# One core, two blocks: layer 1's keys projected for two heads at once, rarer modulation turns, early ScalarE tables, last sums read in place

## The chip, the cores and the metric

The kernel runs on one core of one Trainium2 chip, as a single launch. The metric is the device time of the launch in microseconds (us). Five engines of the core work side by side: TensorE (PE in the profile, with its weight loads as PEld), VectorE (DVE), ScalarE (ACT), GpSimd (POOL) and SyncE (SP), which here only issues the weight transfers.

## The reference

The computation is two model blocks on 256 image tokens ("x") and 256 context tokens ("ctx"), all in float32 with 1024 features. The first block has two layers:

```python
# layer 0: HGRN2 scan in two directions + differential attention, then a routed
#          mixture of 16 experts (top 2) for x and ctx
# layer 1: attention with a window, then a routed mixture for x alone
def odd_layer_mixer(h, hc, w_qkv, w_out, sink, rope, need_ctx):   # layer 1
    p = h @ w_qkv                                  # 16 query heads, 4 key, 4 value heads of 64
    q = p[..., :q_cols].reshape(b_, t_, C_HEADS, C_HEAD_DIM)
    k, v = jnp.split(p[..., q_cols:], 2, axis=-1)
    kvc = hc @ w_qkv[:, q_cols:]                   # context: keys and values alone
    kc, vc = jnp.split(kvc, 2, axis=-1)
    q = apply_axial_rope(q, cos, sin)              # x * cos + rotate_half(x) * sin
    k = apply_axial_rope(k, cos, sin)              # not for kc
    ...                                            # softmax with a sink over kc and a window of k
```

Each layer's norms are modulated by twelve rows that come from `silu(c) @ ada_w` for x and for ctx (shift, scale and gate of mixer and MoE). The second block is a mixer (state space scan and Fourier terms, with a gated norm) and an FFN with experts that choose their tokens. Its result is the last line that matters here: the sum over the experts' tokens goes through an RMS norm (square, mean, root), is multiplied by a gate row and added to x.

## The kernel before

The program of each engine is written out by hand, with a semaphore for each hand-over. Nothing reorders it: an engine runs its instructions in the order in which the code was written, and a wait holds back all that stands behind it on that engine. Stages end at a `meet()`, where PE, ACT and DVE wait for each other.

**Weights.** They stream from HBM through a ring of five slots of 2 MB in SBUF (more in the stages of experts). A piece is 1024 rows by 512 columns of a weight (`piece(key)`), `landed(n)` says that it is there, and SP issues the next transfer (L375) when the slot's last piece has been used up (`used.sem`, read as `consumed`). So the order of the pieces is fixed, and when one is used sets when the slot's next transfer starts.

**HGRN stage** (`hgrn_tensor`, `hgrn_vector`, `hgrn_scalar`). Two directions, four steps each (a step is 128 tokens), are written in turns with the layer's modulation: `in_turns(a, b, mods(...))` takes one turn of each in rotation. For PE a full step has 14 turns: 0, 1 and 10 hold no products of the scan, 2 to 9 hold one level of scores each, 11 the outputs, 12 the transposes, 13 the new state; the last step ends after its turn 11. The modulation is a chain of four units (`u` = 2 to 5). A unit has pieces of `ada_w` (one piece: 8 products of 32 x 512 that go through four column groups of PE) and then one block of sums: DVE copies the four partial sums out of PSUM (L656), PE adds them by two small products, DVE multiplies (L659), and a transfer queued on ACT writes the row out. There are 20 pieces and 4 blocks of sums in all. `mods(one, us)` gives a piece or a block of sums each turn, so that pieces stand at turns 0 to 3, 5 to 8, 10 to 15 and 17 to 22, and sums at 4, 9, 16 and 23: 12 pieces in the first step, 8 in the second, none in the last two.

**Layer 1's projection** (`qkv_tensor`, `qkv_scalar`, `qkv_vector`). `HT` holds the normed activations with features on partitions. PE makes units `u` of eight products into `bank(u % 4)`: units 0 to 7 are queries (two heads of 64 features in the 128 partitions), 8 to 11 keys, 12 to 15 values. A query head in the upper 64 partitions needs its key in the upper half too, so each key unit makes one head's key twice, into partitions 0 to 63 and 64 to 127, by two rounds of eight products that are 64 wide. ACT copies every unit out of PSUM. Between the units PE multiplies queries and keys of x by the rotation matrix (`rope`), and DVE adds up the turned parts (L2311 to L2313). The window attention follows after a `meet()`; it starts with products of `KK` and `QC`.

**Activation tables.** ACT has one set of functions loaded. The compiler puts an ACT_TABLE_LOAD directly ahead of an activation whose function isn't in the set. Whether it runs while ACT would wait for that activation's input, or only behind the wait, is seen in the trace by the idle time ahead of the load and behind it.

**Norms.** `normed(...)` makes squares on ACT, mean on DVE, root on ACT (L489), reciprocal on DVE (L514), then the scaled rows, transposes on PE and modulation. Between layer 1 and the second block `last_norm_vector` / `last_norm_scalar` scale x once more, and the second block's norm `norm2` squares all four chunks of x and ctx (L487).

**Last experts** (`experts_tensor`, `experts_scalar`, `experts_vector`). Pieces of three expert weights stream with wide slots, for four groups of tokens `g`. The sums over experts stay in four PSUM banks over all groups. At the end ACT and DVE copy them to SBUF (L3401, L3428), PE spreads the gate row over 128 partitions by two products (`gate_spread`), ACT squares (L3407) and takes the root (L3409), DVE scales and adds (L3435, L3437), and the result is stored.

## Time and profile before

| what | value |
|---|---|
| timed runs | 3090.97, 3085.37 and 3090.32 us, median 3090.32 us |
| profiled execution | 3081.36 us, of which the span of the engines is 3079.9 us |
| mean granted TensorE clock | 0.913 |
| PE busy | 81% of the span |
| DVE, ACT, POOL busy | 39%, 29%, 3% |
| DMA packets | 819.43 MB, mean 266 GB/s |
| HGRN stage | 142.5 to 333 us |
| layer 1's projection | 1235 to 1332 us |
| layer 1's experts | 1510 to 2010 us |
| last experts | 2587 us to the end |

The table's last rows are places on the time axis of the profiled execution. Rows of the trace give, for a group of instructions, the busy time, the mean duration of one and the idle time ahead of it on its engine with what ended it; rows of the time line give start and duration, and in brackets the idle time before. One float32 product shows as two records on PE (x16 is eight products).

### The profile page before, as it was taken

The page shows a single profiled execution, that of the slowest core. Times are in us where ns is not written, and L with a number is a line of the kernel's source. Part 1 is how long each engine was busy: PE and PEld are TensorE (multiplying, and loading weights), DVE is VectorE, ACT ScalarE, POOL GpSimd, SP SyncE. Part 2 cuts the span into 40 slices and gives each one's busy share as a digit, 9 for nine tenths or more (in the row PEclk, how much of TensorE's full clock was granted, in tenths as well). Part 3 has the DMA queues.
Part 4 walks back from the last instruction along what each step waited for, and adds up shares of the span by engine and source line. Part 5 has one row for each costly group of instructions (what it writes and reads, how often), then busy time and mean ns, then how long its engine had stood idle before and what let it go on. Part 6 is the DMA issues. An engine that isn't in the chain of part 4 may idle for free.

```text
span 3079.9 us, 30001 instructions
## 1 busy us (share of the span) xinstructions
PE 2498.3 (81%) x12205; PEld 1413.4 (46%) x12205; DVE 1207.3 (39%) x2040; ACT 895.6 (29%) x1408; POOL 107.7 (3%) x177
## 2 busy tenths in 40 slices
PE   6875687689999995998587777759898997778777
PEld 4734565578888884543232222234464433222222
DVE  2367537479999995153200000022661012000001
ACT  3334313278887784132100000032131011000000
POOL 1010300100000001000100000000000000000000
PEclk9986798889999997998799999969999998999998
DMA  9393530289999994373799999952102434999996
GB/s 341 123 363 147 201 144 1 95 319 393 389 394 395 393 378 179 132 259 132 274 399 403 398 402 403 372 178 82 41 20 96 164 132 176 409 409 409 409 409 279
DMA packets 246852, 819.43 MB, mean 266 GB/s; under 512 B 11075, under 2 KB 11241, under 8 KB 246448
## 3 DMA queue, kind: packets, MB, share of 16 engines
q1 hardware_dynamic: 226688, 753.88, 63.5%
q0 software_dynamic: 14432, 45.54, 4.3%
q10 hardware_dynamic: 5584, 17.98, 1.5%
q8 instruction: 101, 1.65, 0.2%
q14 instruction: 47, 0.39, 0.0%
HBM read 779.46 MB, written 37.90 MB: 265 GB/s over the span
## 4 chain that ended last, share of the span: by engine, by line
PE 58%; DMA 25%; DVE 10%; ACT 3%; issue 3%; SPq 1%; POOL 0%; DVEq 0%; ACTq 0%; POOLq 0%
PE PS L245 56%; DMA ring<-in_moe_w_up 8%; DMA ring<-in_w_e_down 4%; DMA ring<-in_w_e_up 4%; DMA ring<-in_moe_w_gate 3%; DMA ring<-in_w_e_gate 2%; DMA ring<-in_ada_w 1%; PE PS L1803 1%; DMA ring<-in_moe_w_down 1%; DVE hgrn L949 1%; SPq L375 1%; PE PS L551 0%; DVE SM L1412 0%; DVE SM L2415 0%; DMA row<-YP,DST 0%
## 5 line engine op out<-in xcount | busy, mean ns | idle before, releaser
L411 DVE TENSOR_TENSOR cut<-ring,cut 128x1024 fp32r<-128x1024 f32 x424 | 501.6, 1220 | 178.7 <-ACT cut L403 167.4
L403 ACT CAST cut<-ring 128x1024 fp32r<-128x1024 f32 x424 | 438.2, 1054 | 263.5 <-PE PS L245 237.8
L245 PE MATMUL PS<-cut,xeT 128*128 128x512 f32 x1536 | 364.5, 394 | 3.0 <-DVE cut L411 3.0
L245 PEld LDWEIGHTS PS<-cut,xeT 128*128 128x128 f32 x1536 | 285.9, 189 | 67.2 <-DVE cut L411 5.9
L245 PE MATMUL PS<-ring,hidT 128*64 128x512 f32 (+1 forms) x1024 | 245.3, 630 | 70.7 <-DMA ring<-in_w_e_down 32.3
L245 PE MATMUL PS<-ring,xeT 128*64 128x512 f32 x1024 | 244.9, 628 | 63.5 <-DMA ring<-in_moe_w_gate 34.4
L245 PE MATMUL PS<-ring,XE 128*32 128x512 f32 x1008 | 243.2, 638 | 56.3 <-DMA ring<-in_w_e_up 37.0
L245 PE MATMUL PS<-HT,ring 128*128 128x512 f32 (+2 forms) x576 | 206.9, 527 | 1.2 <-DVE HT L524 1.2
L245 PE MATMUL PS<-cut,hidT 128*128 128x512 f32 x768 | 179.7, 394 | 4.5 <-DVE hidT L1812 4.5
L245 PEld LDWEIGHTS PS<-ring,xeT 128*64 128x64 f32 x1024 | 78.0, 143 | 229.0 <-issue 170.5
L245 PEld LDWEIGHTS PS<-ring,hidT 128*64 128x64 f32 (+1 forms) x1024 | 71.2, 129 | 231.6 <-issue 174.8
L245 PEld LDWEIGHTS PS<-ring,XE 128*32 128x32 f32 x1008 | 71.5, 116 | 221.9 <-issue 220.9
L3422 DVE TENSOR_TENSOR hid<-hid,PS 128x512 f32<-128x512 f32 x8 | 5.1, 683 | 426.6 <-PE PS L245 426.6
L245 PEld LDWEIGHTS PS<-cut,hidT 128*128 128x128 f32 x768 | 146.2, 190 | 35.4 <-DVE hidT L1812 4.7
L245 PEld LDWEIGHTS PS<-HT,ring 128*128 128x128 f32 (+1 forms) x576 | 100.4, 180 | 93.4 <-issue 87.2
L245 PE MATMUL PS<-ring,HT 128*128 128x512 f32 (+2 forms) x384 | 138.0, 520 | 0.7 <-DVEq L181 0.7
L245 PE MATMUL PS<-cut,parts 128*128 128x512 f32 x480 | 115.2, 403 | 21.7 <-DVE cut L411 16.1
L2046 DVE TENSOR_TENSOR hid<-hid,PS 128x512 f32<-128x512 f32 x16 | 11.0, 687 | 307.6 <-PE PS L245 307.6
L245 PE MATMUL PS<-parts,cut 128*128 128x512 f32 x480 | 111.7, 395 | 3.6 <-DVE cut L411 3.6
L245 PEld LDWEIGHTS PS<-cut,parts 128*128 128x128 f32 x480 | 93.8, 196 | 43.0 <-issue 16.3
L245 PEld LDWEIGHTS PS<-parts,cut 128*128 128x128 f32 x480 | 91.8, 192 | 23.0 <-issue 3.7
L245 PE MATMUL PS<-ring,YT 128*128 128x512 f32 x224 | 100.3, 610 | 1.5 <-ACTq L181 0.8
(534 smaller groups left out, 2441.2 us busy)
## 6 DMA issues: line engine op xcount, KB each, us to landing
ring<-in_moe_w_gate SPq DMA_DIRECT2D x64, 2048.0 KB, 12.8
ring<-in_moe_w_up SPq DMA_DIRECT2D x64, 2048.0 KB, 12.4
ring<-in_moe_w_down SPq DMA_DIRECT2D x64, 2048.0 KB, 12.7
ring<-in_w_e_up SPq DMA_DIRECT2D x32, 2048.0 KB, 19.2
ring<-in_w_e_down SPq DMA_DIRECT2D x32, 2048.0 KB, 20.4
ring<-in_w_e_gate SPq DMA_DIRECT2D x31, 2048.0 KB, 18.4
ring<-in_ada_w SPq DMA_DIRECT2D x24, 2048.0 KB, 15.5
ring<-in_w_in SPq DMA_DIRECT2D x13, 2048.0 KB, 7.8
```

The costliest lines, as they stand in the source:

```text
L245: return pe.matmul(o, l, r, start=start, stop=stop, **kw)
L375: sp.dma_start(dst, src).then_inc(landed(n)[0], 16)
L403: act.copy(self.bufs[i % len(self.bufs)][0], w).then_inc(self.high.sem, 1)
L411: dve.tensor_tensor(low, w, high.bitcast(F32), ALU.subtract).then_inc(self.low.sem, 1)
L949: ins = dve.tensor_tensor(level_view(w, l)[:, :, s, :], level_view(of, l)[:, :, s, :], level_view(e, l)[:, :, s, :], ALU.mult)
L1803: last = pe.transpose(bank(6 + t % 2)[:, i * P:(i + 1) * P], src[:, i * P:(i + 1) * P], ident)
L2046: dve.tensor_tensor(hid[i], hid[i], bank(2 + i), ALU.mult).then_inc(B.hidden.sem, 1)
L3422: dve.tensor_tensor(hid[i][:, sl], hid[i][:, sl], bank(6 + h), ALU.mult).then_inc(hidden.sem, 1)
```

## The change

It has five parts.

1. A new `ready_table(func)` activates one column of ones into a spare column, so that the compiler's ACT_TABLE_LOAD comes there. It is called at ten places: ahead of the wait for the mean in the norm after the HGRN stage (`onorm_scalar`) and after differential attention, ahead of the router's sigmoid, at the start of `combine_scalar` and of `owo_scalar`, ahead of the roots of the z norm and of the gate norm in the second block, ahead of the experts' choice and ahead of the last sums.
2. `mods` has a new argument `turns`, and the HGRN stage has a piece or a block of sums of the modulation at every second turn. Pieces stand at 0, 2, 4, 6, at 10, 12, 14, 16, at 20 to 30 and 34 to 44 (even turns), sums at 8, 18, 32 and 46: 6, 6, 6 and 2 pieces in the four steps, and one block of sums in each.
3. The keys of layer 1 are projected by two units of eight products that are 128 wide (two heads together, into `KR`). Ten rotations remain instead of twelve. Four products `double(g)` with a doubled identity (`twice`, made by DVE), 64 partitions deep, bring each head's key into both halves, and DVE copies the four results to `KK`.
4. The squares of `norm2` move into `last_norm_scalar`, in the order ctx (chunks 2 and 3), then x (0 and 1).
5. In the last experts the products of `gate_spread` stand at the start and DVE copies them to `gate_row`. ACT's squares and DVE's scaling read the sums in PSUM, and the copies L3401 and L3428 are gone.

The orders of POOL's and SP's instructions are the same.

```diff
+    def ready_table(func):
+
+        n = readied[0]
+        readied[0] += 1
+        act.activation(column(1856 + n, 1), ones[:, 0:1], func)
...
-    def mods(one, us):
+    def mods(one, us, turns=1):
+
         for u in us:
-            yield from one(u)
+            for _ in one(u):
+                for _ in range(turns):
+                    yield
...
         act.wait_ge(*mod_out(3))
+        ready_table(ACT.Sqrt)
         act.wait_ge(*sq_summed(0))
         act.activation(ss, ss, ACT.Sqrt).then_inc(sq_rooted.sem, 1)
...
+        def double(g):
+
+            pe.wait_ge(*roped(8 + g // 2))
+            if g == 0:
+                pe.wait_ge(*twice_made(0))
+            sl = slice(64 * (g % 2), 64 * (g % 2) + 64)
+            mm(double_bank(g), twice[sl, :, :].rearrange("p a b -> p (a b)"), KR[sl, g // 2, :], True, True).then_inc(doubled.sem, 1)
+
...
-            for half in range(2 if 8 <= u < 12 else 1):
-                for c in range(8):
-                    if u < 8:
-                        last = mm(b[:, 0:256], w[:, c, u % 4 * P:(u % 4 + 1) * P], HT[:, c, 0:256], c == 0, c == 7)
-                    elif u < 12:
-                        last = mm(b[64 * half:64 * half + 64, :], w[:, c, 64 * (u - 8):64 * (u - 7)], HT[:, c, :], c == 0, c == 7)
...
+                elif u < 10:
+                    last = mm(b, w[:, c, P * (u - 8):P * (u - 7)], HT[:, c, :], c == 0, c == 7)
...
+            if u > 11:
+                double(2 * u - 24)
+                double(2 * u - 23)
...
+        for g in range(4):
+            dve.wait_ge(*doubled(g))
+            dve.tensor_copy(KK[:, g, :], double_bank(g))
...
+        act.wait_ge(*x2_in(0))
+        for i, c in enumerate((2, 3, 0, 1)):
+            if i:
+                act.wait_ge(*x2_squared(i - 1))
+            if c < 2:
+                act.wait_ge(*last_normed(c))
+            act.activation(SQ, X[:, c, :], ACT.Square, accum_out=rs2[:, c:c + 1]).then_inc(x2_squared.sem, 1)
...
+        for h in range(2):
+            last = mm(bank(h), ident[0:12, 10:11].to_broadcast([12, P]), MOD[:, h * 512:h * 512 + 512], True, True)
+        last.then_inc(gate_spread.sem, 1)
         for g in range(4):
...
+            if g == 0:
+                pe.wait_ge(*gate_taken(0))
...
+        ready_table(ACT.Sqrt)
         act.wait_ge(*summed(0))
         for c in xc:
-            act.copy(F2[:, c, 512:1024], bank(2 + c)).then_inc(odd_taken.sem, 1)
-        for c in xc:
-            act.wait_ge(*even_taken(c))
-            act.wait_ge(*odd_taken(c))
             if c:
                 act.wait_ge(*f_squared(0))
-            act.activation(hid[0], F2[:, c, :], ACT.Square, accum_out=rs[:, c:c + 1]).then_inc(f_squared.sem, 1)
+            act.activation(hid[0], bank(2 * c, 2), ACT.Square, accum_out=rs[:, c:c + 1]).then_inc(f_squared.sem, 1)
...
-            vs.settle(dve.scalar_tensor_tensor(out=F2[:, c, :], in0=F2[:, c, :], scalar=rs[:, c:c + 1], in1=bank(4, 2),
+            vs.settle(dve.scalar_tensor_tensor(out=F2[:, c, :], in0=bank(2 * c, 2), scalar=rs[:, c:c + 1], in1=gate_row,
                                                op0=ALU.mult, op1=ALU.mult))
```

**PE in the first step of the HGRN stage.** `ring` and `CP` are a piece of the modulation, `hgrn` the levels of the scan (the two directions in rotation), `mod_place` and `KC` the sums. Before:

```order
393 L245 MATMUL PS<-ring_49,CP_55 32x512 x16
394 L245 MATMUL PS<-hgrn_1088 64x64 x4
395 L245 MATMUL PS<-hgrn_1096 64x64 x4
396 L245 MATMUL PS<-ring_49,CP_55 32x512 x8
397 L245 MATMUL PS<-hgrn_1087 32x32 x8
398 L245 MATMUL PS<-hgrn_1095 32x32 x8
399 L245 MATMUL PS<-ring_49,CP_55 32x512 x8
400 L245 MATMUL PS<-hgrn_1088 32x32 x16
401 L245 MATMUL PS<-hgrn_1096 32x32 x16
402 L245 MATMUL PS<-mod_place_63,KC_52 12x512 x2
```

And in the changed kernel:

```order
393 L253 MATMUL PS<-ring_49,CP_55 32x512 x8
394 L253 MATMUL PS<-hgrn_1088 64x64 x4
395 L253 MATMUL PS<-hgrn_1096 64x64 x4
396 L253 MATMUL PS<-ring_49,CP_55 32x512 x8
397 L253 MATMUL PS<-hgrn_1087 32x32 x8
398 L253 MATMUL PS<-hgrn_1095 32x32 x8
399 L253 MATMUL PS<-hgrn_1088 32x32 x16
400 L253 MATMUL PS<-hgrn_1096 32x32 x16
401 L253 MATMUL PS<-ring_49,CP_55 32x512 x8
402 L253 MATMUL PS<-hgrn_1087 32x32 x16
```

A pair of levels without a piece now stands between two pieces, and the sums have moved back by four levels; the empty turn between the last piece and its sums is the pair of levels ahead of them.

**PE at layer 1's keys.** `HT` with `ring` is a projection (queries and keys), `ring` with `HT` the values, `QC`/`KK`/`KR` with `KC` a rotation, `KK` with `QC` the attention's first products. Before:

```order
4014 L245 MATMUL PS<-QC_14053,KC_52 128x256
4015 L245 MATMUL PS<-HT_14051,ring_49 64x512 x16
4016 L245 MATMUL PS<-QC_14053,KC_52 128x256
4017 L245 MATMUL PS<-HT_14051,ring_49 64x512 x16
4018 L245 MATMUL PS<-KK_14054,KC_52 128x256
4019 L245 MATMUL PS<-HT_14051,ring_49 64x512 x16
4020 L245 MATMUL PS<-KK_14054,KC_52 128x256
4021 L245 MATMUL PS<-HT_14051,ring_49 64x512 x16
4022 L245 MATMUL PS<-KK_14054,KC_52 128x256
4023 L245 MATMUL PS<-ring_49,HT_14051 128x256 x8
4024 L245 MATMUL PS<-KK_14054,KC_52 128x256
4025 L245 MATMUL PS<-ring_49,HT_14051 128x256 x24
```

And in the changed kernel:

```order
4018 L253 MATMUL PS<-HT_14055,ring_49 128x512 x8
4019 L253 MATMUL PS<-QC_14057,KC_52 128x256
4020 L253 MATMUL PS<-HT_14055,ring_49 128x512 x8
4021 L253 MATMUL PS<-KR_14059,KC_52 128x256
4022 L253 MATMUL PS<-ring_49,HT_14055 128x256 x8
4023 L253 MATMUL PS<-KR_14059,KC_52 128x256
4024 L253 MATMUL PS<-ring_49,HT_14055 128x256 x16
4025 L253 MATMUL PS<-KR_14059,twice_14060 128x512 x2
4026 L253 MATMUL PS<-ring_49,HT_14055 128x256 x8
4027 L253 MATMUL PS<-KR_14059,twice_14060 128x512 x2
4028 L253 MATMUL PS<-KK_14058,QC_14057 128x512 x2
```

Sixty-four products of 64 x 512 have become sixteen of 128 x 512, and four small ones stand between the last values and the attention.

**ACT from the combination of layer 1's experts to the second block's norm.** Before:

```order
1112 L2207 ACTIVATE row_18476<-row_18476,SM_56 128x1024
1113 L2207 ACTIVATE row_18478<-row_18478,SM_56 128x1024
1114 L2212 ACTIVATE SQ_58,XS_57<-X_50 128x1024 x2
1115 L2547 ACT_TABLE_LOAD
1116 L2547 ACTIVATE XS_57<-XS_57 128x2
1117 L487 ACTIVATE SQ_58,SM_56<-X_50 128x1024 x4
1118 L489 ACTIVATE SM_56<-SM_56 128x4
```

And in the changed kernel:

```order
1118 L243 ACT_TABLE_LOAD
1119 L243 ACTIVATE SM_56<-ones_53 128x1
1120 L2222 ACTIVATE row_18430<-row_18430,SM_56 128x1024
1121 L2222 ACTIVATE row_18432<-row_18432,SM_56 128x1024
1122 L2227 ACTIVATE SQ_58,XS_57<-X_50 128x1024 x2
1123 L2586 ACTIVATE XS_57<-XS_57 128x2
1124 L2593 ACTIVATE SQ_58,SM_56<-X_50 128x1024 x4
1125 L497 ACTIVATE SM_56<-SM_56 128x4
```

The table load has moved from behind the last squares of the combination to ahead of its first rows; the four squares keep their place in the row, with other waits and another order of chunks.

## Rows read from the trace of the kernel before

**Rows 1.** The page: the chain that ended last, by engine.

```profile
PE 58%; DMA 25%; DVE 10%; ACT 3%; issue 3%; SPq 1%; POOL 0%; DVEq 0%; ACTq 0%; POOLq 0%
```

**Rows 2.** Stretches: length, PE, PEld, DVE, ACT, POOL busy, PEclk, DMA share, GB/s.

```profile
1268.00:1350.00 82.00, 79.55 (x304) 34.27 (x303) 19.13 (x54) 13.68 (x36) 0.00 (x0) 1.00 0.28 101
1350.00:1430.00 80.00, 66.94 (x421) 29.99 (x419) 47.28 (x134) 34.50 (x101) 5.03 (x10) 0.91 0.71 264
...
1510.00:2010.00 500.00, 389.23 (x1722) 129.84 (x1723) 33.11 (x48) 19.54 (x32) 7.72 (x15) 0.95 0.99 385
```

**Rows 3.** The same view, the four steps of the HGRN stage.

```profile
142.50:197.20 54.70, 39.74 (x656) 18.30 (x656) 34.85 (x84) 21.45 (x53) 9.77 (x20) 0.88 0.92 330
197.20:254.30 57.10, 39.47 (x643) 22.29 (x641) 36.19 (x91) 22.37 (x55) 2.95 (x6) 0.88 1.05 387
254.30:296.20 41.90, 20.54 (x486) 18.46 (x487) 33.67 (x89) 21.84 (x55) 0.00 (x0) 0.61 0.15 54
296.20:333.00 36.80, 18.92 (x468) 16.68 (x466) 30.04 (x81) 18.57 (x50) 0.00 (x0) 0.56 0.01 2
```

**Rows 4.** Time lines of PE and DVE, in the HGRN stage; PE's waits from 170 to 240.

```profile
154.37 3.54 PE L245 MATMUL PS<-ring,CP 128*32 128x512 f32 x16
...
193.54 1.92 PE L245 MATMUL PS<-ring,CP 128*32 128x512 f32 x16
...
160.36 0.69 DVE L656 COPY mod_place<-PS 128x512 f32<-128x512 f32 x1 [2.00 <-PE PS L245]
163.13 0.74 DVE L659 SCALAR_TENSOR_TENSOR mod_place<-PS,KC,mod_place 12x512 f32<-12x512 f32 x1 [2.08 <-PE PS L245]
...
PE PS L245 <- issue: 5.5, 2, 2.9
PE PS L245 <- DMA ring<-in_ada_w: 3.4, 3, 2.4
```

**Rows 5.** Time line of PE at layer 1's keys; a full-width unit in the chain.

```profile
1266.37 12.29 PE L245 MATMUL PS<-HT,ring 128*64 128x512 f32 x32
...
1317.66 3.62 PE L245 MATMUL PS<-ring,HT 128*128 128x256 f32 x16
...
1332.66 1.13 PE L245 MATMUL PS<-KK,QC 64*128 64x512 f32 x4 [0.59 <-ACTq L181]
...
2100.42 6.87 PE PS L245 x16
```

**Rows 6.** ACT's table loads by line: busy, mean ns, idle ahead of them.

```profile
L489 ACT ACT_TABLE_LOAD x3 | 3.8, 1283 | 0.8 <-DVE XS L506 0.8
...
L1158 ACT ACT_TABLE_LOAD x1 | 1.3, 1283 | 11.3 <-DVE SM L1168 11.3
...
L3148 ACT ACT_TABLE_LOAD x1 | 1.3, 1283 | 0.0
```

**Rows 7.** Time line of ACT at the last norm, and at the gate norm.

```profile
2026.18 1.28 ACT L2547 ACT_TABLE_LOAD   x1 [0.41 <-DVE XS L2537]
...
2030.42 1.06 ACT L487 ACTIVATE SQ<-X 128x1024 bf16<-128x1024 f32 x1 [2.75 <-DVE X L2542]
...
2035.35 0.20 ACT L489 ACTIVATE SM<-SM 128x4 f32<-128x4 f32 x1 [0.24 <-DVE SM L506]
...
2535.05 0.59 ACT L3141 COPY SB<-PS 128x512 f32<-128x512 f32 x1 [13.15 <-PE PS L245]
```

**Rows 8.** Time line at the end of the program.

```profile
3067.07 1.07 ACT L3401 COPY F<-PS 128x512 f32<-128x512 f32 x2 [3.30 <-PE PS L245]
3067.08 1.29 DVE L3428 COPY F<-PS 128x512 f32<-128x512 f32 x2 [42.46 <-PE PS L245]
```

**Rows 9.** Start of the last experts (PE, SP), and their stretch as in rows 2.

```profile
2587.55 13.04 PE L245 MATMUL PS<-ring,XE 128*32 128x512 f32 x61 [0.76 <-ACTq L181]
...
2594.61 0.37 SPq L375 DMA_DIRECT2D ring<-in_w_e_gate  x1
...
2640.00:3040.00 400.00, 315.48 (x1303) 95.14 (x1301) 10.29 (x16) 6.48 (x12) 0.00 (x0) 0.94 1.03 409
```

More of the change, by code:

```diff
@@ L2204, in combine_scalar @@
         def combine_scalar():
+            ready_table(ACT.Sqrt)
             for i in range(nch):
@@ L2242, in program @@
     KK = chunked(room("KK", 2048, 6144), 4)
+    KR = chunked(room("KR", 1024, 9216), 2)
+    twice = two(room("twice", P, 10240))
     VC = chunked(room("VC", 1024, 8192), 4)
@@ L2252, in program @@
     swa_in, sink_in = S.new("window_in", "pool_q", 16), S.new("sink_in", "pool_q", 16)
-    projected, rope_made = S.new("projected", "pe"), S.new("rope_made", "pe")
+    projected, rope_made, doubled = S.new("projected", "pe"), S.new("rope_made", "pe"), S.new("doubled", "pe")
+    twice_made = S.new("twice_made", "dve")
     raw, roped = S.new("raw", "act"), S.new("roped", "dve")
@@ L2302, in qkv_scalar @@
             else:
-                act.copy(qkv_dst(u), bank(u % 4)[:, 0:512 if u < 12 else 256]).then_inc(raw.sem, 1)
+                act.copy(qkv_dst(u), bank(u % 4)[:, 0:512 if u < 10 else 256]).then_inc(raw.sem, 1)
     def qkv_vector():
-        for r in range(12):
+        dve.tensor_tensor(twice, ident[:, 0:64].unsqueeze(1).to_broadcast([P, 2, 64]),
+                          ident[:, 64:P].unsqueeze(1).to_broadcast([P, 2, 64]), ALU.add).then_inc(twice_made.sem, 1)
+        for r in range(10):
             a = qkv_dst(r)[:, 0:256]
@@ L2477, in owo_scalar @@
     def owo_scalar():
+        ready_table(ACT.Sqrt)
         for c in xc:
@@ L2547, in last_norm_scalar @@
         act.activation(XS[:, 0:2], XS[:, 0:2], ACT.Sqrt).then_inc(last_rooted.sem, 1)
+        act.wait_ge(*x2_in(0))
[5 more added lines that the diff above has]
+            act.activation(SQ, X[:, c, :], ACT.Square, accum_out=rs2[:, c:c + 1]).then_inc(x2_squared.sem, 1)
+    rs2, x2_squared = small(8), S.new("x2_squared", "act")
     last_norm_vector()
@@ L2551, in program @@
     S.retire(1, last_scaled, last_rooted)
+    S.retire(4, x2_squared)
     HT = chunked(room("HT", 8 * 512, 0), 8)
@@ L2563, in program @@
     Y2 = XH[:, 2:4, :]
-    rs2 = small(8)
     DT, U, DA, AC, NA, EA, WS, ET = (small(192) for _ in range(8))
@@ L2950, in z_scalar @@
             act.activation(zz[c], bank(k), ACT.Silu).then_inc(z_silu.sem, 1)
+        ready_table(ACT.Sqrt)
         for c in xc:
@@ L3135, in gate_scalar @@
             act.activation(gt2[c], bank(k), ACT.Sigmoid).then_inc(gate_sig.sem, 1)
+        ready_table(ACT.Sqrt)
         for t in (1, 3):
@@ L3273, in choice_scalar @@
     def choice_scalar():
+        ready_table(ACT.Exp)
         act.wait_ge(*shifted(0))
@@ L3384, in experts_tensor @@
                 for c in xc:
-                    last = mm(bank(2 * h + c), SWT[:, g, c * P:(c + 1) * P], YE[:, g, h * 512:h * 512 + 512], g == 0, g == 3)
+                    last = mm(bank(2 * c + h), SWT[:, g, c * P:(c + 1) * P], YE[:, g, h * 512:h * 512 + 512], g == 0, g == 3)
         last.then_inc(summed.sem, 1)
-        for h in range(2):
-            last = mm(bank(4 + h), ident[0:12, 10:11].to_broadcast([12, P]), MOD[:, h * 512:h * 512 + 512], True, True)
-        last.then_inc(gate_spread.sem, 1)
     def experts_scalar():
```

51 lines of the change are left out of this document (30 added, 21 removed).

## The prediction

> **What bounds the kernel now.** The page's chain says that the end is set by PE for 58% of the span, by transfers for 25%, by DVE for 10% and by ACT for 3% [rows 1]. Such shares are means over stages that differ, so I read next the view by stretches. Where layer 1's keys are made PE is busy all the time at a granted clock of 1.00 and the transfers are mostly idle (share 0.28), while layer 1's experts have a transfer share of 0.99 [rows 2] and the last experts 1.03 [rows 9]. So PE work saved at the keys counts in full, and PE work inside an experts' stage counts for nothing. The HGRN stage differs again: in its first two steps PE, DVE and the transfers are all busy, in the last two the transfers stand still, PE has under 21 us of work in some 40, and the granted clock falls to 0.61 and 0.56, which is mostly the lower level of 1.2 GHz [rows 3]. There a chain of small hand-overs between PE, DVE and ACT sets the time. Everything else that the change touches is a few microseconds at a stage's seam, where one engine works and the others wait; for these I read the time line of the engine.
>
> **Layer 1's keys: -33.5 us.** The sixteen 64-wide products of one key take 12.29 us as the records show, and from the first key to the first value unit there are four periods, (1317.66 - 1266.37) / 4 = 12.82 us each, so the rotation between them takes 0.53 [rows 5]. A unit of eight full-width products with 512 columns takes 6.87 us [rows 5]; a 64-wide round of eight costs nearly as much (12.29 / 2 = 6.1), since the columns streamed are the same. So two new units with their rotations take 2 x (6.87 + 0.53) = 14.8 us in the place of 51.3, which is 36.5 less. Against this stand the four doubling products. They are 64 partitions deep, write 128 x 512 and come in pairs on the two halves, just as the pair of attention products at 1332.66, which takes 1.13 us [rows 5]: 2.3 us for both pairs. DVE's four copies of 128 x 512 cost 1.29 / 2 = 0.65 each, by the two of the same shape at the end [rows 8]; the first two run beside PE's last value unit (3.62 us), the last two start as PE ends, 1.3 us. There ACT's copy of the last values was already waited for (0.59 idle ahead of the first attention product [rows 5]), so 0.7 is new. Sum: -36.5 + 2.3 + 0.7 = -33.5. DVE's doubled identity and the rotations of the second key unit are made beside the values. The bounds: if pairs don't overlap, each product costs an eighth of a unit, 0.86, and the doubling 3.4; if moreover PE waits before the first for DVE's three operations on the last rotation (1.3 by copies' size), the sum is -31; if all copies are hidden, -34.2. Downstream the window attention is moved forward as a block. Its pieces of modulation need their slots free, which they get when the projection's pieces are used up, and those are now used up 33 us earlier too; the transfers are at rest for most of the stage [rows 2], so nothing is late next.
>
> **The HGRN stage: -7 us.** The unknown is what modulation costs among the scan's hand-overs. The last two steps hold none: 41.9 and 36.8 us [rows 3]. Three full steps and the short last one would be at most 3 x 41.9 + 36.8 = 162.5, and four times their mean 157.4; I take 160. The stage takes 190.5 (54.7 + 57.1 + 41.9 + 36.8), so 20 pieces and 4 blocks of sums cost some 30 us. A block of sums costs DVE the copy 0.69, an idle 2.08 for PE's two products and 0.74 for the multiplication, 3.5 us in which the scan stands [rows 4], and four of them are 14 us that stay, whatever their turn. Of the other 16, waits of PE for the pieces' transfers and for issue are 3.4 + 5.5 = 8.9 us between 170 and 240 [rows 4], and the other 7 are pieces whose 1.92 us didn't fit beside DVE's work, with the 2.00 that DVE idled ahead of L656 for a piece written directly ahead of it [rows 4]. With two turns to a piece, 6 pieces a step need 6 transfers in 55 us instead of 12, so the waits for transfers go, and DVE finds the last piece done when it comes to the copy. What stays is the pieces in the tail of a step, where the scan waits for PE alone: turn 8 twice and turn 12 three times, five pieces of 1.92, 9.6 us. After: 14 + 9.6 = 23.6 against 30.5, -7. Below, if the tail's pieces are hidden as well: -16. Above: the pieces in steps 3 and 4 now stand where the clock was at its lower level, and there a piece takes 3.54 [rows 4]; if the lower level holds over the tail's five pieces it adds 8, and over the products of the sums (2.08 of DVE's idle is theirs) 4 x 2 = 8 more, +9. I take the middle value because the pieces themselves fill PE, and in the two steps that had them it was granted 0.88 [rows 3].
>
> **Early tables: -2.7 us.** A load takes 1.283 us [rows 6]. It pays to move it only where it ran behind the wait or behind work of its own chain. The norm after HGRN: ACT idled 11.3 us, and then loaded [rows 6]: -1.3. The first norm of layer 1's mixer (L489, idle 0.8 ahead of a load): between 0 and -1.3, as DVE also waits there for the modulation's transposes; -0.5. The gate norm: ACT idled 13.15 us ahead of its last copy [rows 7], and the load came behind the squares without a gap [rows 6]; it goes into the idle time, -1.3 and 0.2 for the new activation if that is late: -1.1. The z norm: the load stood directly behind ACT's two squares, and now stands ahead of them, behind the same SiLU, so only its place in ACT's queue changes, and the added activation costs 0.2, as the root of the same kind does [rows 7]. Attention, routers, choice and `owo_scalar`: the load already ran in idle time or another wait ends later, 0. The trace shows no time between a load and its activation: in the last norm the load starts at 2026.18, and 4.24 us later, with the load's 1.28, the root, a reciprocal, one scaling of x and their hand-overs behind it, the first square already runs [rows 7]. The Trainium skill ("ScalarE: Activation LUTs", What ACT_TABLE_LOAD costs) gives a drain of some 1.38 us beside the 1.283 for each switch; by that the five places on the path (these three, the last norm and the last sums) would give 7 us more, 3036, an estimate from that page. The load's length agrees with the trace.
>
> **The last norm: -3.9 us.** The load goes from behind the mean to ahead of the combination (-1.3) [rows 7]. The four squares ran from 2030.42 to just ahead of the root at 2035.35, 1.17 us each, after ACT had idled 2.75 us for DVE's scaling of x [rows 7]. The two of ctx don't need that scaling and now fit in the idle time, so some 2.6 of it is won. Bounds: -2.5 (the ctx chunks come late) and -4.2.
>
> **The last experts: 0.** At the end ACT's copies (from 3067.07, 1.07) leave the chain [rows 8] and so does a load (1.283) [rows 6], some 2.0 to 2.3 with the new readying activation in idle time. But at the start two products of the gate row and their hand-over stand ahead of the first piece at 2587.55. SP issued its first transfer into a freed slot at 2594.61, when the first piece was used up, and from there the transfers ran at a share of 1.03 almost to the end [rows 9]. So what stands ahead of 2587.55 moves the whole stage: two products of 12 x 512, as those between L656 and L659, 2.0 [rows 4]. I take +2.0 and -2.0. Ends: -2 and +1.
>
> **The sum.** -33.5 - 7 - 2.7 - 3.9 + 0 = -47.1. Against the profiled execution, 3081.36, that is 3034.3. The median of the timed runs lies 9 us above the profiled one, so against 3090.32 it is 3043.2, and I predict 3043.
>
> **Rivals.** (a) Clock and tail in the HGRN stage: rarer pieces only move the work to steps at the lower level, so the stage gets longer by up to 9. For it: 0.61 and 0.56 [rows 3], and 3.54 for a piece [rows 4]. Then -47.1 + 16 = -31, 3059. (b) Every load is worth its time, the six at 0 or above as well, and the tail's pieces of HGRN are hidden: 6 x 1.3 + 9.6 = 17 more, 3026. Against it: ACT has 3% of the chain [rows 1], and loads at a seam mostly ran while ACT would have idled. (c) The change at the keys doesn't show, since the experts of layer 1 are bound by transfers (0.99) that can't start earlier: then 33.5 fall out, 3077. Against it: they start when slots come free, and these are freed by PE, whose work has moved; the transfers are far from full here (0.28) [rows 2]. (d) Slower: with less PE work at the keys the clock falls to 1.2 GHz from the doubling products on and stays through the window attention. PE has 33 us less at a granted 1.00 [rows 2] and is then interrupted by softmax. The stretch with the attention (1350 to 1430) holds 66.94 us of PE work [rows 2]; if that doubled and some 60 us of it lay on the path, the time would be 3043 + 60 = 3103. It decides once more than 47 us of the added PE time show at the end. Against it: both stretches were granted 1.00 and 0.91 [rows 2], the second with PE interrupted by softmax already.
>
> **Chances.** Forecast as worked out, within some 7 us: 0.70. (a) 0.16, (b) 0.06, (c) 0.04, (d) 0.01; 0.03 is left for what isn't listed. The range must leave out 0.2 at most: it goes from 3031 (the low ends of HGRN and of the tables) to 3059 (case a). The likely time lies far from 3090, and 0.2%, about 6 us, is what a measurement of this kernel can tell from no change. Only (d) is slower, and only part of the rest is within 6 us: faster 0.97, same 0.02, slower 0.01.
>
> **What would show it.** Right: from the first key to the first attention product about 33 us in place of 66.3; two units of about 6.9 us; steps of the HGRN stage of about 50, 50, 48 and 37 us with no PE wait for `ada_w`; a load in ACT's idle time ahead of the norms' roots; the four squares of the last norm beginning while DVE still scales x. Wrong: the HGRN steps summing to over 195 us at a granted clock of 0.6 would be (a); a longer wait of PE for `moe_w_gate` or for the router's transfers that takes back the keys' gain would be (c); 12 us or more lost between the projection and the router at 0.5 of the clock would be (d); an end that is shorter by 2 us, with a start of the last experts that is not later, would make the term of the gate row wrong.

## The result

The changed kernel takes 3045.23 us (median of four runs, 3042.81 to 3047.03) against 3088.77 us of the kernel before (four runs, 3085.37 to 3090.97). The ratio is 0.986, with a 95% interval of 0.9842 to 0.9877, so the change makes it some 43 us faster. 3043 us was predicted. Run once more beside others it took 3043.33 us against 3085.55 (below). The profiled execution has a span of 3044.7 us against 3079.9, which is only 35.2 us less. That difference between medians and profiles has to be explained too.

The profile after, first the page's chain, which answers [rows 1]:

```profile
PE 58%; DMA 25%; DVE 10%; issue 3%; ACT 2%; SPq 1%; POOL 1%; DVEq 0%; PEldq 0%; ACTq 0%; POOLq 0%
```

The shares are those of before within 1%; a change of 1.4% that lies in a dozen places hardly moves them. One sees it stretch by stretch. PE's time line at layer 1's keys answers [rows 5]:

```profile
1265.31 7.03 PE L253 MATMUL PS<-HT,ring 128*128 128x512 f32 x16
...
1279.90 3.62 PE L253 MATMUL PS<-ring,HT 128*128 128x256 f32 x16
...
1290.79 1.13 PE L253 MATMUL PS<-KR,twice 64*128 64x512 f32 x4
...
1298.04 1.13 PE L253 MATMUL PS<-KK,QC 64*128 64x512 f32 x4 [1.41 <-DVEq L181]
```

From the first key to the first attention product there are 32.7 us where there were 66.3. Two units end at 1279.90, after 14.6 us in the place of 51.3. A pair of doubling products takes 1.13 us, as the attention's pair did, and PE idles 1.41 us for DVE's last two copies and the meeting instead of 0.59.

The four steps of the HGRN stage (columns as in [rows 2]; the steps' ends are those of the new state's update), which answer [rows 3]:

```profile
142.50:193.20 50.70, 33.65 (x571) 16.00 (x564) 33.17 (x81) 21.24 (x53) 6.76 (x14) 0.73 0.60 212
193.20:241.90 48.70, 32.97 (x595) 18.05 (x597) 34.70 (x89) 22.56 (x55) 2.95 (x6) 0.79 0.74 264
241.90:291.50 49.60, 31.75 (x592) 18.11 (x588) 35.05 (x91) 22.04 (x55) 2.96 (x6) 0.79 0.73 262
291.50:330.50 39.00, 21.92 (x500) 14.70 (x492) 31.35 (x83) 18.61 (x50) 0.00 (x0) 0.69 0.42 151
```

The sum is 188.0 us against 190.5. The first two steps have become 4.0 and 8.4 us shorter, the third and fourth 7.7 and 2.2 longer. DVE's busy time is the same (134 us). The granted clock has moved between the steps. In the first two it is 0.73 and 0.79 where it was 0.88, which is a larger share of the lower level of 1.2 GHz; in the last two it is 0.79 and 0.69 where it was 0.61 and 0.56. Over the whole stage it is 0.76 in both kernels, and PE's busy time there has hardly changed, 120.3 us against 118.7. So the pieces, which had all stood in the first two steps, became dearer, and the scan's own products cheaper by nearly as much. These are the groups of the pieces' products in the stage, before and after (columns as in [rows 6], and PE's waits as in [rows 4]):

```profile
L245 PE MATMUL PS<-ring,CP 128*32 128x512 f32 x320 | 43.5, 665 | 6.1 <-DMA ring<-in_ada_w 3.4 <-DVEq L181 2.6
```

```profile
L253 PE MATMUL PS<-ring,CP 128*32 128x512 f32 x320 | 54.2, 808 | 2.6 <-DVEq L181 2.6
```

The same products took 54.2 us of PE where they took 43.5, and the 3.4 us of waits for `ada_w` are gone.

The loads of ACT moved as written. The last norm's root (which answers [rows 7]) and the end of the program (which answers [rows 8]):

```profile
1993.78 0.20 ACT L2586 ACTIVATE XS<-XS 128x2 f32<-128x2 f32 x1 [0.42 <-DVE XS L2576]
1993.89 1.04 ACT L2593 ACTIVATE SQ<-X 128x1024 bf16<-128x1024 f32 x1
...
1998.80 0.21 ACT L497 ACTIVATE SM<-SM 128x4 f32<-128x4 f32 x1 [0.23 <-DVE SM L514]
...
3030.77 1.28 ACT L243 ACT_TABLE_LOAD   x1
3032.06 0.20 ACT L243 ACTIVATE SM<-ones 128x1 f32<-128x1 f32 x1
3034.05 1.02 ACT L3456 ACTIVATE hid<-PS 128x1024 f32<-128x1024 f32 x1 [1.79 <-PE PS L253]
```

The mean's root stands directly ahead of the squares of ctx, with no load and no idle time between, and from the mean's root to the norm's root there are 5.02 us where there were 7.89 (2035.35 less the end of the load, 2026.18 + 1.28, in [rows 7]). At the end the load is over before the sums are, and the squares start as they end.

The start of the last experts, PE and SP, answers [rows 9]:

```profile
2552.47 1.95 PE L253 MATMUL PS<-MOD,KC 12*128 12x512 f32 x4 [0.80 <-ACTq L181]
2554.35 6.20 PE L253 MATMUL PS<-ring,XE 128*32 128x512 f32 x28
...
2561.43 0.37 SPq L383 DMA_DIRECT2D ring<-in_w_e_gate  x1
```

The gate row's products stand ahead of the first piece and take 1.9 us, and the first freed slot is refilled 7.1 us after that piece, as before.

### The profile page after: what moved, and what is told of

It reads as the page before. It is cut to its first block, busy times and chain, and to the rows that moved or that the text cites. A ratio compares the mean times of both kernels' runs of the same rounds, so it can differ in the third digit from the quotient of the medians.

```text
span 3044.7 us, 29818 instructions
## 1 busy us (share of the span) xinstructions
PE 2459.1 (81%) x12113; PEld 1394.1 (46%) x12113; DVE 1207.5 (40%) x2038; ACT 895.4 (29%) x1415; POOL 108.8 (4%) x177
## 4 chain that ended last, share of the span: by engine, by line
PE 58%; DMA 25%; DVE 10%; issue 3%; ACT 2%; SPq 1%; POOL 1%; DVEq 0%; PEldq 0%; ACTq 0%; POOLq 0%
PE PS L253 55%; DMA ring<-in_moe_w_up 8%; DMA ring<-in_w_e_down 5%; DMA ring<-in_w_e_up 3%; DMA ring<-in_moe_w_gate 3%; DMA ring<-in_w_e_gate 2%; PE PS L1817 1%; DVE hgrn L957 1%; DMA ring<-in_moe_w_down 1%; SPq L383 1%; DMA ring<-in_ada_w 1%; PE PS L559 0%; DVE SM L2453 0%; DMA SM<-in_router_w 0%; DMA row<-YP,DST 0%
## 5 line engine op out<-in xcount | busy, mean ns | idle before, releaser
L253 PE MATMUL PS<-ring,hidT 128*64 128x512 f32 (+1 forms) x1024 | 240.0, 618 | 73.7 <-DMA ring<-in_w_e_down 37.1
L253 PE MATMUL PS<-ring,XE 128*32 128x512 f32 x1008 | 235.3, 618 | 62.3 <-DMA ring<-in_w_e_up 40.9
L253 PE MATMUL PS<-HT,ring 128*128 128x512 f32 (+1 forms) x480 | 171.0, 511 | 1.2 <-DVE HT L532 1.2
L253 PE MATMUL PS<-cut,parts 128*128 128x512 f32 x480 | 116.2, 405 | 20.4 <-DVE cut L419 14.8
L253 PEld LDWEIGHTS PS<-HT,ring 128*128 128x128 f32 x480 | 90.5, 192 | 68.4 <-issue 62.1
L2047 ACT ACTIVATE hid<-PS 128x512 f32<-128x512 f32 x16 | 9.6, 597 | 314.5 <-PE PS L253 314.5
L253 PEld LDWEIGHTS PS<-ring,HT 128*128 128x128 f32 x384 | 71.3, 204 | 67.2 <-issue 64.0
```

The lines of the kernel that those rows point to most:

```text
L253: return pe.matmul(o, l, r, start=start, stop=stop, **kw)
L2047: act.activation(hid[i], bank(i), ACT.Silu).then_inc(B.silu.sem, 1)
```

## The experiments

All comparisons are with the kernel before, run on the same chip in the same set. Its medians in the four sets were 3085.55, 3087.78, 3086.63 and 3086.80 us. The changed kernel itself ran in the first set alone, so in the others a difference from it is one between two gains over the kernel before. Medians of a few runs differ by 1 to 2 us on their own, and single executions by 5 us and more. So I read each kernel's median beside the length of its HGRN stage (from the first piece to DVE's squares behind the stage) in its profiled execution.

### The changed kernel once more, and every turn again

The first is the changed kernel itself. The second undoes part 2 alone:

```diff
-    in_turns(hgrn_tensor(0), hgrn_tensor(1), mods(mod_tensor, range(2, 6), turns=2))
+    in_turns(hgrn_tensor(0), hgrn_tensor(1), mods(mod_tensor, range(2, 6)))
```

and the same for DVE and ACT.

> The changed kernel itself once more, as the base for the three others of this set. All theories: 0.986 of the kernel before, some 3045 us. If the 35 us between the two profiled executions are the truth and the 43.5 us of the medians are scatter, it should lie nearer 3050.

Measured: 3043.33 us against 3085.55, ratio 0.9867 (0.9852 to 0.9882), 42.2 us faster. The gain of the medians is there again, and so the 35 us between the first two profiles is for the most part scatter of single executions; its own profiled execution had a span of 3040.8.

> The changed kernel with the modulation at every turn of the HGRN stage again (part 2 undone alone). Theory of the prediction (waits for transfers and DVE's idle ahead of the copy are saved, pieces in a step's tail cost 1.92 us each): 7 us slower than the changed kernel. Rival, by the traces of the two kernels (the stage went from 190.5 to 188.0 us, since the granted clock fell to 0.73 to 0.79 in the first three steps and most pieces now take 3.0 to 3.6 us): 2 to 3 us slower. If the gain is taken up again by the attention's transfers or the experts, 0.

Measured: 3050.13 us, ratio 0.9885 (0.987 to 0.99), 6.8 us above the changed kernel. By the medians the prediction's 7 us stands. The stages say less. With pieces at every turn the stage took 190.8 (before), 192.1 (keys alone, below) and 192.1 us (this one), mean 191.7; with pieces at every second turn 188.4, 188.7, 191.1, 188.8 and 190.2 us in the five kernels that leave it as changed (after, its repeat, without tables, norm as before, late gate row), mean 189.4. That is 2.3 us, with groups that just overlap, and a difference of medians with intervals of some 5 us each can't decide between 2.3 and 7.

### Sums spread over two turns

DVE copies the partial sums, goes on with a turn of the scan, and multiplies then; ACT waits a turn later too.

```diff
+    def split_vector(u):
...
+        dve.wait_ge(*consumed(W.at[tag, js[-1], h]))
+        dve.tensor_copy(sums, mod_banks(u)[0]).then_inc(mod_taken.sem, 1)
+        yield
+        o = MOD[:, 512 * h:512 * h + 512] if dst is None else GB
+        dve.wait_ge(*mod_summed(u))
...
```

> The changed kernel with a block of sums spread over two turns on DVE and ACT: DVE copies the partial sums, does a turn of the scan, and multiplies then; PE's order is the same. If the 2.1 to 3.2 us that DVE idles for PE's two products are on the path (as the prediction says of all 3.5 us), four blocks give 8 to 9 us. If PE's own time for the products is what the scan waits for, it gives 0 to 2 us.

Measured: 3035.46 us, ratio 0.9843 (0.983 to 0.9857), 7.9 us below the changed kernel, with a stage of 183.7 us, 5.7 less than the mean of 189.4. DVE's time line, first of the changed kernel, then of this one:

```profile
208.45 0.68 DVE L664 COPY mod_place<-PS 128x512 f32<-128x512 f32 x1
...
211.39 0.74 DVE L667 SCALAR_TENSOR_TENSOR mod_place<-PS,KC,mod_place 12x512 f32<-12x512 f32 x1 [2.26 <-PE PS L253]
```

```profile
208.55 0.70 DVE L1140 COPY mod_place<-PS 128x512 f32<-128x512 f32 x1
...
212.09 0.73 DVE L1144 SCALAR_TENSOR_TENSOR mod_place<-PS,KC,mod_place 12x512 f32<-12x512 f32 x1
...
L253 PE MATMUL PS<-ring,CP 128*32 128x512 f32 x320 | 55.7, 828 | 2.6 <-DVEq L181 2.6
```

The idle 2.26 us between copy and multiplication are filled with the scan's work. DVE's idle time on PE's two products was on the path, as the prediction's term for a block of sums says. The expectation of 8 to 9 us is met by the median (7.9) and not by the stage (5.7). The pieces took 55.7 us of PE here, a little more than in the changed kernel, and yet the stage is shorter: their sum on PE isn't what sets its length.

### Pieces at the turns in which PE has nothing of the scan

Pieces at a step's turns 0, 1 and 10, sums at turn 3:

```diff
+    MOD_AT = (0, 0, 1, 1, 3, 10, 14, 14, 15, 17, 24, 24, 28, 28, 29, 29, 31, 38, 38, 42, 42, 43, 43, 45)
...
```

> The changed kernel with the same pieces and sums of modulation at other turns of the HGRN stage: pieces by two to four at a step's turns 0, 1 and 10, in which PE has no products of the scan, and sums at turn 3. If the tail's pieces (turns 8 and 12) cost their time, as the prediction says, 9 us faster than the changed kernel (3043.3 us against 3085.6 in the first set). If the clock is what counts (longer stretches of small products at the lower level), no gain or a loss of up to 5 us. If bursts of pieces outrun the transfers, PE waits for them again and the gain is under 4 us.

Measured: 3040.87 us against 3087.78, ratio 0.9855 (0.9837 to 0.9872); 46.9 us faster, where the changed kernel had 42.2 and 43.5. The stage took 187.2 us, 2.2 less than the mean, not 9. No wait for `ada_w` came back. The group of the pieces, and a block of sums:

```profile
L253 PE MATMUL PS<-ring,CP 128*32 128x512 f32 x320 | 43.1, 691 | 2.6 <-DVEq L181 2.6
...
201.12 0.69 DVE L664 COPY mod_place<-PS 128x512 f32<-128x512 f32 x1
205.59 0.74 DVE L667 SCALAR_TENSOR_TENSOR mod_place<-PS,KC,mod_place 12x512 f32<-12x512 f32 x1 [3.78 <-PE PS L253]
```

The pieces are back at 43.1 us, and the sums now fall among the scan's small products alone, with up to 3.78 us of idle time for DVE where it was 2.08 to 3.18 (12.4 us for the four where it was 9.9): the granted clock was 0.71 over the stage. More of what the tail gave was paid elsewhere. These are DVE's waits for PE in the stage (in total, how many, the longest) ahead of the new state's update and of the outputs, first in the changed kernel, then in this one:

```profile
DVE hgrn L1005 <- PE PS L253: 10.5, 2, 5.3
DVE hgrn L1001 <- PE PS L253: 5.3, 1, 5.3
DVE O L984 <- PE PS L253: 5.2, 2, 4.2
DVE O L987 <- PE PS L253: 4.5, 3, 2.3
```

```profile
DVE O L984 <- PE PS L253: 9.6, 2, 5.9
DVE O L987 <- PE PS L253: 9.0, 3, 4.5
DVE hgrn L1005 <- PE PS L253: 4.2, 2, 2.3
DVE hgrn L1001 <- PE PS L253: 2.9, 1, 2.9
```

Without a piece at turn 12 the update was waited for 8.7 us less (7.1 for 15.8), which is near the 9 that was expected. But the outputs were waited for 8.9 us more (18.6 for 9.7). PE has nothing of the scan at turn 10, but the outputs stand right behind it, and the pieces put there hold them up.

### Part 3 alone, part 1 and part 4 undone

The kernel before with the keys' change alone; the changed kernel with `ready_table` empty; the changed kernel with the four squares back in `norm2`:

```diff
-        act.activation(column(1856 + n, 1), ones[:, 0:1], func)
+        return
```

```diff
...
-    norm2 = normed(allc, 0, 2, H, HT, rs2, None, there=(x2_squared(3),), mod_there=(mod_there,))
+    norm2 = normed(allc, 0, 2, H, HT, rs2, SQ, there=(last_normed(1), x2_in(0)), mod_there=(mod_there,))
```

> The kernel before with part 3 alone, the keys of layer 1. The prediction: 33.5 us faster than before (ratio 0.989). If the rest of the change gives the difference, by what the two profiles showed for it (33.6 us at the keys, 35.2 in all), the same; if layer 1's experts take it up, which are bound by transfers, under 10 us.

Measured: 3050.65 us, ratio 0.9878 (0.9861 to 0.9894), 37.1 us faster than before. From the norm's reciprocal to the attention's first DVE operation its profile has 72.9 us against 106.8 before and 73.4 in the changed kernel. The gain is neither taken up by layer 1's experts nor needs the rest of the change. Its profiled execution was 6.3 us longer than its median; 4.1 us more than before lie between the last norm and the gate norm (515.9 us against 511.8), where nothing was changed.

> The changed kernel without the ten readied tables. The prediction: 2.7 us for the three seams, 1.3 for the last norm and 1.3 at the end, so 5.3 us slower than the changed kernel. If a drain as long again as the load went with each switch that was on the path (the Trainium skill, ScalarE: Activation LUTs, What ACT_TABLE_LOAD costs), some 12 us slower. If the loads were hidden by other waits, 0.

Measured: 3048.46 us, ratio 0.9876 (0.986 to 0.9893); 39.3 us faster than before, 3 to 4 us less than the changed kernel's 42 to 43.5. That is nearest to the 5.3 us, but with intervals of some 5 us on both the medians alone don't exclude 0 either. The profiles give it place by place: without the readied tables the norm after HGRN takes 1.3 us longer, layer 1's first norm 0.6, the last norm 1.3, the gate norm 1.1 and the end 1.1, while the z norm takes 0.5 less, 4.9 us in all. Part of it was made up by something else: the experts' choice took 17.8 us from the gate norm's reciprocal to its own where it took 19.8 in the changed kernel, since the router's products ran at a granted 0.99 where it was 0.61:

```profile
2516.80:2523.00 6.20, 3.94 (x39) 2.65 (x38) 2.13 (x9) 3.88 (x8) 0.00 (x0) 0.99 0.96 369
```

In the changed kernel's time line above the load ends at 3032.05 and the activation starts at 3032.06, so a drain isn't seen.

> The changed kernel with the squares of the second block's norm where they were (part 4 undone alone). The prediction: 2.6 us slower than the changed kernel. If the ctx squares don't fit into ACT's idle time, 0 to 1 us.

Measured: 3044.90 us, ratio 0.9857 (0.9841 to 0.9874); 42.9 us faster than before, no difference from the changed kernel that medians show. The profiles do show it: with the squares back the norm's root comes 7.9 us after the mean's root, as before, where it came after 5.0. 2.6 us is below what these runs resolve.

### Does the clock eat the gain?

Extra products at PE's empty turns keep PE busy:

```diff
+    def filler(n):
+        for _ in range(n):
+            mm(bank(7)[64:128, :], ident[:, 0:64], KC[:, 0:512], True, True)
...
+            filler(3)
             yield
             for i in range(10):
+                if i in (0, 9):
+                    filler(2)
```

> The changed kernel with extra products in the HGRN stage whose results nobody reads: of each direction three at a step's turn 0, two at turn 1 and two at turn 10, in which PE has no products of the scan, 56 in all. They compute nothing that the kernel needs and leave nothing out. If the granted clock is what eats the gain of part 2 (0.73 to 0.79 in the first steps of the changed kernel, pieces of 3.0 to 3.6 us), PE's fuller work brings it back towards 0.9, pieces go back to 1.9 us and the stage gets 3 to 6 us shorter in spite of the added work. If the clock is of no account because DVE and the hand-overs set the scan's pace, the stage keeps its 188 to 189 us or gets longer by the products that don't fit, up to 10 us.

Measured: 3063.38 us against 3086.63, ratio 0.9912 (0.9895 to 0.9929), some 20 us slower than the changed kernel. Its six executions lie in two groups, four at 3063.25 to 3065.87 us and two at 3051.47 and 3052.49, and the profiled one (3063.51) is of the first. The stage of this kernel, and then that of the changed one (columns as in [rows 2]):

```profile
142.50:345.00 202.50, 159.34 (x2360) 76.80 (x2360) 134.22 (x340) 84.11 (x210) 12.76 (x26) 0.87 0.59 210
```

```profile
142.50:330.70 188.20, 120.29 (x2248) 66.86 (x2240) 134.30 (x340) 84.45 (x210) 12.68 (x26) 0.76 0.63 225
```

The clock did come back, 0.87 against 0.76, and the pieces fell to 45.3 us of PE. But the added products took 51.0 us, PE's busy time rose by 39 us, and the stage became 14 us longer. So the granted clock follows PE's work here, as expected, and the work that buys it cost more than it gave back. Where it was paid is seen in DVE's waits:

```profile
DVE O L984 <- PE PS L253: 14.3, 2, 8.4
DVE O L987 <- PE PS L253: 11.3, 3, 5.9
```

The outputs were waited for 25.6 us in the place of 9.7, behind the products added at turn 10. So this run shows the price of their place above all, and what the clock alone would be worth isn't told apart by it.

### The late gate row, and what adds up

The gate row's products behind the first group's gate pieces; then with spread sums; then with spread sums and the other turns:

```diff
-        last.then_inc(gate_spread.sem, 1)
         for g in range(4):
...
             for j in (0, 2):
                 pair(4, XE, g, j, "g")
+            if g == 0:
+                for h in range(2):
+                    last = mm(bank(h), ident[0:12, 10:11].to_broadcast([12, P]), MOD[:, h * 512:h * 512 + 512], True, True)
+                last.then_inc(gate_spread.sem, 1)
```

> The changed kernel with the gate row's products of the last experts behind the first group's gate pieces. The prediction says that what stands ahead of the first piece moves the stage, which is bound by transfers, by 2.0 us: 2 us faster. If the two products ran while the first piece was awaited anyway: 0.

Measured: 3045.38 us, ratio 0.9864 (0.9849 to 0.9878): 41.3 us faster than before, no gain over the changed kernel in the median. The time line has the first piece directly behind the meeting, and the first freed slot follows as soon:

```profile
2552.56 17.83 PE L253 MATMUL PS<-ring,XE 128*32 128x512 f32 x90 [0.76 <-ACTq L181]
...
2559.62 0.37 SPq L383 DMA_DIRECT2D ring<-in_w_e_gate  x1
```

From the gate norm's reciprocal to that of the last norm the kernels with the late row took 532.8, 530.6 and 530.8 us, the changed kernel and its repeat 533.1 and 533.0. In two of three profiles the 2 us are there, in one only 0.2 of them.

> The changed kernel with sums spread over two turns and the late gate row, pieces at every second turn. By the first set's 7.9 us and 2 us: 10 us faster than the changed kernel. If the first set's gain was partly scatter (5.5 us shorter HGRN stage in its profiled execution): 7 us.

Measured: 3031.86 us, ratio 0.9828 (0.9815 to 0.9842). That is 54.8 us below the kernel before, 11 to 13 more than the changed kernel, where 10 was expected, and 7 if part of the earlier gain was scatter.

> The changed kernel with three alterations: sums spread over two turns, the pieces at a step's turns 0, 1 and 10, and the gate row's products of the last experts behind the first group's gate pieces instead of ahead of them. If the gains of the first two add up (7.9 and 4.0 us) and the third gives 2: 14 us faster than the changed kernel, some 3030 us. If split sums and other turns save the same idle time of DVE: 8 plus 2 us, 3034.

Measured: 3034.47 us, ratio 0.9831 (0.9818 to 0.9843), with the shortest HGRN stage of all, 180.4 us against 183.5 of the kernel with spread sums and late gate row. The time is that of the second expectation (3034) and not of the first (3030). The two kernels can't be told apart by their times. Both are faster than either of the two kernels compared here, 52 to 55 us below the one before and 9 to 13 us more than the change gave.

> The changed kernel with pieces at every turn again and the sums spread over two turns: the missing corner of a square of four kernels (pieces at every turn or every second; sums in one turn or in two). If the two act on different idle time, it lies 7 us above the kernel with spread sums alone (some 3042 us) and its HGRN stage is 186 us. If rarer pieces only help because DVE no longer waits for the piece directly ahead of its copy, and spread sums give that as well, it lies within 3 us of the kernel with spread sums alone.

Measured: 3039.22 us against 3086.80, ratio 0.9844 (0.9831 to 0.9857), 47.6 us faster, with a stage of 188.2 us. The square, as microseconds below the kernel before, and the stage's length:

| pieces | sums in one turn | sums in two turns |
|---|---|---|
| every turn | 35.4, 192.1 us | 47.6, 188.2 us |
| every second turn | 42.2, 188.7 us | 50.1, 183.7 us |

Rarer pieces give 6.8 and 2.5 us by the medians and 3.4 and 4.5 by the stages; spread sums 12.2 and 7.9, and 3.9 and 5.0. By the stages each effect shows with the other in place, as if they acted on different idle time. By the medians this run lies 2.5 us above the kernel with spread sums alone, which is within the 3 us that the rival expectation named. The medians and stages agree on the sign, not on the size, so which of the two expectations holds stays open.

## Why the prediction was right, and where its terms were off

The time was right to 2 us, and the range (3031 to 3059) held it. That it came so close is in part luck. The gain was forecast at 47.1 us and measured at 43.5 and 42.2; the absolute time was worked out from a median of 3090.32 us for the kernel before, and with its fourth run that median is 3088.77. The terms can be followed by aligning DVE's instructions in the two profiles and reading how the distance between them moves:

| term | predicted | measured in the profiles |
|---|---|---|
| layer 1's keys | -33.5 | -33.4 |
| HGRN stage | -7 | -2.3 (means of stages), -2.5 to -6.8 (medians) |
| table, norm after HGRN | -1.3 | -1.3 |
| table, layer 1's norm | -0.5 | -0.6 |
| last norm, table and squares | -3.9 | -4.1 |
| z norm | +0.2 | +0.4 |
| gate norm | -1.1 | -1.2 |
| last experts | 0 | +0.5 |
| sum | -47.1 | -42.0 |

**The keys** came out as worked out: 14.6 us for two units and their rotations (14.8 predicted), 2.3 for the doubling pairs, 0.8 for the copies (0.7 predicted). No engine and no transfer took its place, since the stage was PE's alone. Rivals (c) and (d) are refuted: 37.1 us in the median with this part alone, and a granted clock of 1.00 and 0.93 over the keys and the attention behind them:

```profile
1266.00:1300.00 34.00, 32.59 (x125) 19.94 (x126) 7.48 (x17) 2.66 (x6) 0.00 (x0) 1.00 0.27 95
1300.00:1400.00 100.00, 84.96 (x525) 36.85 (x518) 61.10 (x172) 45.83 (x131) 5.13 (x10) 0.93 0.72 263
```

**The HGRN stage** is the term that was mis-sized, -7 for a measured -2.3. Its steps came out nearly as forecast (50, 50, 48 and 37 were expected, 50.7, 48.7, 49.6 and 39.0 measured), and what was to be saved was saved: PE's waits for `ada_w` went, and so did the 7.4 us that DVE had idled ahead of its copies. DVE's waits for PE in the stage before (the changed kernel's are those at L1005 and L1001 above, and for the sums the row below):

```profile
DVE mod_place L659 <- PE PS L245: 8.4, 4, 2.1
DVE mod_place L656 <- PE PS L245: 7.4, 3, 4.0
DVE hgrn L997 <- PE PS L245: 5.0, 2, 2.9
DVE hgrn L993 <- PE PS L245: 3.7, 1, 3.7
```

```profile
DVE mod_place L667 <- PE PS L253: 9.9, 4, 3.2
```

What was priced too low is what stays. The step that failed is "I take the middle value because the pieces themselves fill PE". At every second turn they don't: the granted clock of the first steps fell to 0.73 to 0.79, and a piece that had taken 1.92 us took 2.8 to 3.6 wherever it stood alone among the levels. The three pieces at turn 12 had been put at 5.8 us, and the updates behind them were waited for 8.7 us longer than in the kernel that has no piece there (15.8 us in this profile and 16.8 to 17.2 in the four others with this order, against 7.1); the idle time at the four sums had been put at 8.3 us and was 9.9. That is 4.5 us or more above what was priced, about the 4.7 by which the term was off. The figures come from single profiles, and no run changed the clock alone, so that the lower clock made these places dear is argued and not shown.

It is the mechanism of rival (a) in those two places and not in the stage as a whole, whose granted clock stayed at 0.76: the scan's own products became cheaper as the pieces became dearer. The forecast also left out turn 10, since PE has nothing of the scan there. Moving pieces to it showed that they hold up the outputs behind it. The price of the sums was right in kind: spreading them saved 5.7 us of stage.

**The tables** were worth about their load where the rows of before showed an idle time or a chain ahead of it, 4.9 us in all by the profiles. Rival (b) needed 3026 us, and the interval of the ratio ends at some 3040. By the figures that the Trainium skill gives ("ScalarE: Activation LUTs", What ACT_TABLE_LOAD costs) the same edit would have been worth some 12 us, an estimate from that page. The load's 1.283 us is the trace's, the drain isn't.

**The last experts** were even, but not exactly: at the start the products cost 1.9 us of PE, and +1.6 to +1.9 us show at the first group; the end gave back 2.2. The remaining 0.6 stands between the gate norm and the first piece, in both profiles of the changed kernel. Half of it is at the router, where the logits' products took 0.87 us for 0.53, at a granted clock of 0.61 around them where it was 0.67; for the other half I found no cause.

**Profiles and medians.** The sum of the terms, -42.0, is near that of the medians (-43.5 and -42.2) and not the -35.2 of the two profiled executions. One place where the difference lies is layer 0's projection behind attention, in which nothing was changed. PE's time line there, before and after:

```profile
521.45 3.67 PE L245 MATMUL PS<-MOD,KC 12*128 12x512 f32 x8 [0.66 <-DVE parts L1515]
```

```profile
517.33 5.72 PE L253 MATMUL PS<-MOD,KC 12*128 12x512 f32 x8 [0.65 <-DVE parts L1528]
```

The same eight records took 5.72 instead of 3.67 us, the granted clock up to the next cut of weights was 0.64 instead of 0.85, and 3.3 us were lost. In the repeat of the changed kernel the records took 5.48 us, and 1.7 us were lost. This is no rare accident: of the fourteen profiled executions four had 3.67 us there (before, keys alone, without tables, extra products) and the ten others 4.69 to 5.72. So it can be a cost that the change itself brings, and not scatter; no run settles it. The rest of the 7 us is some 2 us between layer 1's attention and the last norm, a stretch whose experts are bound by transfers and which took between 691.1 and 696.0 us, from DVE's first operation of the attention, in the fourteen profiled executions, and smaller pieces.

## What to carry to other kernels

Eight products that fill 64 partitions cost PE 6.1 us here, and eight that fill 128 cost 6.9, so what is made in two rounds of 64 is worth trying in one round of 128 and a cheap copy into the other half, wherever PE alone sets the time. In a chain of small hand-overs look at what an engine waits for between two of its own instructions: putting one turn of other work there was worth at least as much as thinning out the work beside it. A turn in which an engine has nothing of the chain isn't free if the chain's next product stands right behind it. And of a table load the time counted that the trace showed behind a wait or in the middle of a chain.

## What the runs showed of the hardware that I had not expected

The granted clock followed the work that PE had in each step. With the same 20 pieces spread out it moved from 0.88, 0.88, 0.61 and 0.56 in the four steps to 0.73, 0.79, 0.79 and 0.69, and the products of the pieces took 54.2 us instead of 43.5, while over the stage it was 0.76 both times. With the pieces bunched at PE's empty turns it was 0.71, and with added products, 51 us of PE, 0.87. The same eight records in the same order took 3.67 us in some kernels and up to 5.72 in others, with a granted clock of 0.85 and 0.64 around them, so a few microseconds between two profiles of this kernel need a look at such places before they are put down to the change. And squares of 128x1024 cost ACT no more when they read two banks of PSUM (1.02 us) than from SBUF (1.06 us before).
